# Joining two factors on VectorE, splitting with the bias, and moving the residual's scaling to GpSimd at one layer boundary

## The reference

```
# end of the first block, 512 tokens, 2048 channels
x = (ALPHA1*xl + g*out - mu) * rsqrt(var + eps) * ln_g + ln_b     # layer norm
# start of the second block
h    = x * (1 + scale) + shift
proj = h @ w_in_2            # q k v gate, glu_a glu_b g_conv
...
x = layer_norm(ALPHA*x + gate*y)                                  # x is needed again: the residual
```

## Time and profile before

| | |
|---|---|
| three runs | 3251.26, 3254.66, 3254.66 us, median 3254.66 |
| the profiled execution | 3252.81 us, its span 3251.2 us |
| mean granted TensorE clock | 0.994 |
| TensorE matmuls busy | 3180.1 us, 98% |
| VectorE busy | 2236.8 us, 69% |
| ScalarE busy | 1346.4 us, 41% |
| GpSimd busy | 294.1 us, 9% |
| moved | 556.41 MB, 171 GB/s |

### The profile page before, as it was taken

How to read it: one execution, slowest core, us unless ns; L and a number is a source line. 1 busy time by engine, 2 the same in 40 slices (tenths; PEclk the granted TensorE clock), 3 DMA queues, 4 the chain that set the end, 5 groups by cost and what they waited for, 6 DMA issues and landing times.

```text
span 3251.2 us, 47549 instructions
## 1 busy us (share of the span) xinstructions
PE 3180.1 (98%) x16736; PEld 2607.7 (80%) x16736; DVE 2236.8 (69%) x3562; ACT 1346.4 (41%) x2085; POOL 294.1 (9%) x521
## 2 busy tenths in 40 slices
PE   7999999999999999999999999999998999999997
PEld 4799999888777777889888777777786888788886
DVE  3488778766777776687556777774676999655446
ACT  2435564432444445246322444444326222454423
POOL 0000002011011101100101000000112000000002
PEclk9999999999999999999999999999999999999999
DMA  9765558556444444655755444432553322222333
GB/s 398 285 237 200 201 187 298 195 207 217 158 149 158 152 138 165 230 176 200 260 192 196 154 147 139 161 113 81 205 211 129 130 90 100 90 86 88 104 118 103
DMA packets 112092, 556.41 MB, mean 171 GB/s; under 512 B 17984, under 2 KB 22128, under 8 KB 69072
## 3 DMA queue, kind: packets, MB, share of 16 engines
q1 hardware_dynamic: 52000, 350.25, 30.2%
q0 software_dynamic: 59952, 204.29, 18.8%
HBM read 531.33 MB, written 23.09 MB: 171 GB/s over the span
## 4 chain that ended last, share of the span: by engine, by line
PE 80%; DVE 9%; DMA 4%; ACT 3%; issue 2%; DVEq 2%; ACTq 0%; POOLq 0%; POOL 0%; SPq 0%
PE acc L1453 23%; PE acc L1455 22%; PE acc L1454 22%; PE pv L1640 3%; DVE w_lo L2026 2%; PE S L1614 2%; DMA xy<-in_wm 2%; PE S L1629 1%; DMA gates<-in_wm 1%; DVE gates L2079 1%; DMA raw<-in_w 1%; PE misc L1543 1%; ACT w_hi L746 1%; ACT work L746 1%; DVE vtok L2079 1%
## 5 line engine op out<-in xcount | busy, mean ns | idle before, releaser
L1453 PE MATMUL acc<-h_hi,w_hi 128*128 128x512 f32 (+1 forms) x4448 | 1623.1, 365 | 12.9 <-DVE w_lo L2026 9.0
L1455 PE MATMUL acc<-h_hi,w_lo 128*128 128x512 f32 (+1 forms) x4448 | 1593.1, 358 | 0.0
L1454 PE MATMUL acc<-h_lo,w_hi 128*128 128x512 f32 (+1 forms) x4448 | 1591.4, 358 | 0.0
L1453 PEld LDWEIGHTS acc<-h_hi,w_hi 128*128 128x128 f32 x4448 | 841.3, 189 | 161.1 <-issue 34.1
L1454 PEld LDWEIGHTS acc<-h_lo,w_hi 128*128 128x128 f32 x4448 | 841.9, 189 | 124.7 <-issue 6.7
L1455 PEld LDWEIGHTS acc<-h_hi,w_lo 128*128 128x128 f32 x4448 | 841.0, 189 | 124.6
L2026 DVE TENSOR_TENSOR w_lo<-raw,w_hi 128x1024 fp32r<-128x1024 f32 x584 | 689.1, 1221 | 178.4 <-ACT w_hi L746 174.2
L746 ACT ACTIVATE w_hi<-raw 128x1024 fp32r<-128x1024 f32 x584 | 585.3, 1053 | 66.0 <-PE acc L1508 18.5
L746 ACT ACTIVATE ev<-acc 128x512 f32<-128x512 f32 (+1 forms) x202 | 106.9, 533 | 804.4 <-PE acc L1455 788.9
L541 POOL DMA_DIRECT2D gates<-in_wm x288 | 153.7, 534 | 1363.7 <-DVE gates L2079 1238.8
L746 ACT ACTIVATE work<-S,small 128x768 f32<-128x768 f32 (+1 forms) x160 | 129.1, 814 | 257.7 <-DVE small L2195 257.7
(11 more groups left out here) (308 smaller groups left out, 2673.1 us busy)
## 6 DMA issues: line engine op xcount, KB each, us to landing
raw<-in_w SPq DMA_DIRECT2D x288, 1024.0 KB, 5.0
gates<-in_wm POOLq DMA_DIRECT2D x288, 512.0 KB, 4.8
xy<-in_wm SPq DMA_DIRECT2D x32, 1024.0 KB, 11.2
raw<-in_wp SPq DMA_DIRECT2D x4, 1024.0 KB, 12.6
x_d<-xy POOLq DMA_DIRECT2D x1, 4096.0 KB, 15.3
qb<-x_d POOLq DMA_DIRECT2D x16, 256.0 KB, 4.1
kb<-x_d POOLq DMA_DIRECT2D x16, 256.0 KB, 4.7
bias_d<-kb POOLq DMA_DIRECT2D x8, 384.0 KB, 20.2
```

The lines of the kernel that those rows point to most:

```text
L1453: mm(o, w_hi[:, w], h_hi[:, x], start=n == 0, stop=False)
L1454: mm(o, w_hi[:, w], h_lo[:, x], start=False, stop=False)
L1455: last = mm(o, w_lo[:, w], h_hi[:, x], start=False, stop=n == len(ks) - 1)
```

## The change

For each of the 16 tiles at this boundary VectorE now multiplies by gain and inverse deviation in one instruction and writes the product to a bank of `S` (four buffers); ScalarE only adds the bias while rounding into `h_hi`; VectorE adds the bias again while subtracting `h_hi` for `h_lo`. The whole modulated tile is written nowhere. The x tiles stay unscaled, and GpSimd multiplies them by a copy of the inverse deviation in `qb` (it can't read PSUM), which ScalarE makes by a second Exp. GpSimd's subtraction of the mean starts at tile 2 instead of 4. The half weight split moves ahead of the statistics. The loops over pairs on VectorE and ScalarE become straight code.

```diff
-        whole_glu = (S[:, 2 * SEQ:3 * SEQ], S[:, 3 * SEQ:4 * SEQ])
+        scaled_glu = [S[:, SEQ * n:SEQ * (n + 1)] for n in (2, 3, 0, 1)]
@@ GpSimd
-            for k in range(4, KT):
+            for k in range(2, KT):
                 x = tile(xy, k, SEQ)
                 nc.gpsimd.tensor_tensor(x, x, t1[:], ALU.subtract).then_inc(rest_done, 1)
+            pool.wait_ge(b_dev_kept, shown(b_dev_kept, 1))
+            for k in (*range(8, KT), *range(8)):
+                x = tile(xy, k, SEQ)
+                pool.wait_ge(n_ready, shown(n_ready, LN_AT["b"] + k + 1))
+                nc.gpsimd.tensor_tensor(x, x, qb[:], ALU.mult).then_inc(b_normed, 1)
@@ ScalarE, norm_affine
-                    act.wait_ge(n_ready, shown(n_ready, At(LN_AT[c] + 1, 1, i)))
+                    if c == "b":
+                        act.wait_ge(b_normed, shown(b_normed, At(-7 if first >= 8 else 9, 1, i)))
+                    else:
+                        act.wait_ge(n_ready, shown(n_ready, At(LN_AT[c] + 1, 1, i)))
@@ ScalarE, boundary
                     inverse_deviation("b", pv)
+                    f(qb[:], t2[:], ACT.Exp, scale=-0.5).then_inc(b_dev_kept, 1)
-            modulate("g.h", lambda i: tile(xy, i, SEQ), SEQ, lambda k: vec("c0", k), lambda k: vec("c1", k),
-                     normed=LN_AT["b"], to=whole_glu)
+            for k in range(KT):
+                act.wait_ge(n_ready, shown(n_ready, LN_AT["b"] + k + 1))
+                f(inputs("g.h", h_hi, k), scaled_glu[k % 4], ACT.Identity, bias=vec("c1", k)).then_inc(hhi_done, 1)
@@ VectorE, end of project_out
                     dve.sem_inc(ssum_ready, 1)
+                    if c == "b":
+                        lo(At(TILE0["glu"] + 1), (1,))
@@ VectorE, boundary
-                    for k in range(4):
+                    for k in range(2):
                         x = tile(xy, k, SEQ)
                         stt(x, stats[0], -1.0 / D, x, ALU.mult, ALU.add)
             dve.wait_ge(ln_sd, shown(ln_sd, LN_NO["b"] + 1))
             dve.drain()
-            scaled(0, 2, pv)
-            def next_pair(i):
-                dve.wait_ge(rest_done, shown(rest_done, At(-2, 2, i)))
-                scaled(i * 2, 2, pv)
-                modulated("g.h", SEQ, i - 1, whole_glu)
-            loop(dve, 1, 4, next_pair)
-            lo(At(TILE0["glu"] + 1), (1,))
-            loop(dve, 4, KT // 2, next_pair)
-            modulated("g.h", SEQ, KT // 2 - 1, whole_glu)
+            def scaled_and_gained(k):
+                if k >= 2:
+                    dve.wait_ge(rest_done, shown(rest_done, k - 1))
+                stt(scaled_glu[k % 4], tile(xy, k, SEQ), vec("c0", k), pv[:, :], ALU.mult, ALU.mult).then_inc(n_ready, 1)
+            def shifted_low(k):
+                dve.wait_ge(hhi_done, shown(hhi_done, H_AT["g.h"] + k + 1))
+                stt(inputs("g.h", h_lo, k), scaled_glu[k % 4], vec("c1", k), inputs("g.h", h_hi, k).bitcast(F32),
+                    ALU.add, ALU.subtract).then_inc(hlo_done, 1)
+            scaled_and_gained(0)
+            scaled_and_gained(1)
+            for k in range(KT):
+                shifted_low(k)
+                if k + 2 < KT:
+                    scaled_and_gained(k + 2)
```

More of the change, by code:

```diff
@@ L297, in build @@
         n_ready = sem("n_ready")
+        b_dev_kept = sem("b_dev_kept")
+        b_normed = sem("b_normed")
         x_ready = sem("x_ready")
```

## The result

| | before | after |
|---|---|---|
| median | 3253.11 us (18 runs, 3249.54 to 3255.11) | 3260.26 us (18 runs, 3258.00 to 3262.57) |
| ratio | | 1.0022, 95% interval 1.0016 to 1.0028 |
| profiled execution, its span | 3252.81, 3251.2 us | 3258.00, 3256.4 us |

The change makes the kernel 7 us slower (5 to 9 by the interval). I had forecast 3249.0, in a range up to 3255.

What follows compares the result with a forecast made beforehand. TensorE bounds the kernel, its matmuls filling 98% of the span. The profiled 3252.81 less 4.8 plus 0.1 already in the dates gave 3248.0, the median of runs 3249.9; the middle, 3249.0, was taken, range 3245.5 to 3255.

Steps and rivals of the forecast that it cites:

- Start and pace: At the boundary: first factor product starts at 2471.05, 0.9 earlier; VectorE's new instructions follow at 0.67, 1.34 us per tile.
- The moved split: Half weight split ahead of VectorE's statistics: 0.14 late for the mean, counted as +0.1 us.
- The sign that I had named: Before the first product, TensorE's wait for `h_lo` would be 4.8 instead of 6.7 us if the forecast was right.
- First matmul with all inputs ready: TensorE's third weight tile would start at 2498.05 instead of 2502.83, a gain of 4.8 us.
- Low clock hidden at the start: TensorE's first blocks: two slow ones from 2473.54 end at 2476.7, the next two fit before k = 4.
- Splits of the third weight tile: On VectorE beside GpSimd's multiplications: up to 1.24 each, first half ready by 2496.4, needed by TensorE at 2498.05.
- Rival C: VectorE's new instructions wait for GpSimd's running one, 1.26 per spacing: 12.4 us slower, 3266; chance 0.05.
- The store and the first taps: GpSimd's first store goes at 2505.4 or so, lands in about 5 us, with 5 us of cover before ScalarE's taps.
- VectorE's free time: At the first taps, VectorE's tenth of free time would take in any shortfall of the store's cover; nothing counted.
- The timed size: Whole kernel: a gain of 4.8 us, time 3249.0, counted as within what a measurement can't tell from no change.

Runs made afterwards that it cites:

- two pauses: Changed kernel with GpSimd resting before tiles 14 and 4 until the third and fourth weight tiles are split, first store moved ahead of the second rest; 3249.49 against 3252.82 us.
- two drains: Changed kernel with a GpSimd drain before its multiplications of tile 14 and of tile 4; 3249.97 against 3254.55 us.
- the six changed versions: Changed kernel without GpSimd's multiplications, or with one pause, two pauses, a drain after each, one short rest or two drains; ratios to the kernel before 0.9987 to 0.9995.
- one version: Changed kernel with one GpSimd wait before its seventh multiplication (tile 14) until the third weight tile is split; ratio 0.9992 to the kernel before.
- the one without multiplications: Changed kernel with GpSimd's 16 multiplications left out, their semaphore still counted; 3248.99 us against 3253.97.
- small kernels: Separate kernels computing nothing of the reference: VectorE weight splits asked for during GpSimd bursts of 6, 24 or 30; plain bursts of 30 gave 2.27 or 19.35 us.
- eight more reads: Kernel before with eight more GpSimd subtractions (two SBUF inputs, results unused) behind its twelve; ratio 1.0023.
- a drain after each: Changed kernel with a GpSimd drain after each multiplication; ratio 0.9995 to the kernel before.

## Why the prediction was wrong

- **Start and pace: right.** First product 5.39 us after GpSimd's start (forecast 2473.54 - 2468.2 = 5.34), 0.66 per instruction (0.67). VectorE's write to PSUM costs nothing that shows, and reading from there neither. The moved split delayed the mean by 0.2 us as forecast (0.14, though the terms that I gave add up to 0.07), but only against an execution whose sums ran at the lower clock, as the one did that I read. Against sums at 1.00 it is 1.1 us. The sign that I had named, a wait of TensorE for `h_lo` of 4.8 us instead of 6.7, hangs on the same thing: 6.5 in the profile of the changed kernel, whose sums ran at 1.00, and 4.8 in the two versions whose sums ran slow (two pauses, two drains).
- **First matmul with all inputs ready: right but for the split.** Forecast 29.85 after GpSimd's start; 29.74 to 29.77 in the six changed versions in which the split isn't kept out.
- **Low clock hidden at the start: right.** By the same 29.75. The forecast did not have its return after the wait.
- **"Splits of the third weight tile (2494 to 2497) meet the multiplications, at up to 1.24 each ... ready by 2496.4": the step that failed.** I took one instruction of GpSimd's as the most that a VectorE instruction waits. It waited for ten. The two rows that I went by had the split asked for in the last instruction of its burst, where one instruction's wait is all that can be seen, or an addition inside a burst of five, which the later runs show to be too short. That the conflict exists I had; how long it lasts I had from nothing, and I gave it no bound from above. The rows for that bound were there: GpSimd's own end, 2505.4 in my dates, plus 1.22 = 2506.6 against a need of 2498.05, so 8.6 us of wait (measured 8.6), and 2.0 for the clock. GpSimd's row of the burst of five, in the kernel before:

```profile
3230.76 2.87 POOL L739 TENSOR_SCALAR xy<-xy,vecs 128x256 f32<-128x256 f32 x5 [2.95 <-DVE xy L2574]
```

- **Rival C: the right place, the wrong instruction.** I looked for the conflict in the new pair, whose one SBUF tensor plus per-channel operand doesn't conflict (0.66 beside a busy GpSimd), and not in the old split behind it, which had got a busy neighbour.
- **The store and the first taps:** the store went at 2504.5, near my 2505.4. Its cover is thin, though. Pausing GpSimd used it up, 4.1 us of wait in one version, and VectorE's free time didn't take that in as I had said: the version ends 2.7 us later than the one without multiplications.
- **The timed size.** -4.8 forecast; the profile has +5.9, being -5.0 + 8.8 (the third tile's delay, nearly all of it the wait) + 2.1 (clock and the like). The 18 timed runs have +7.2, which the interval (5 to 9) joins to it.

The Trainium skill ("SBUF — State Buffer", "Who interferes with whom") has the shared port held for a whole instruction by whoever comes first, the other blocking. The rows of the small kernels agree for up to 14 of GpSimd's instructions since a rest or drain (2.35 us at most, against 1.21 alone). From 15 on the next instruction too goes ahead of VectorE, to the end of the burst (28.5 us at most). The measurement decides.

## What to carry to other kernels

When work moves to an idle engine, look not only at whether that engine keeps up and at the instructions written for it, but at every instruction that shares a port with it and now runs at the same time; put the end of the whole burst, not one instruction, as the upper bound. A long GpSimd burst with SBUF reads wants a drain or a short rest every ten instructions or so, placed ahead of the moment at which VectorE has two-SBUF-input work that TensorE waits for. And a wait of TensorE costs more than itself: here 8.6 us brought 2 more at the lower clock.

## What the runs showed of the hardware

- A VectorE instruction with two SBUF inputs, asked for while GpSimd runs instructions with SBUF inputs back to back, gets in after the running one if that is at most the 15th since GpSimd's last rest or drain, and after the burst's end otherwise: 2.27 against 19.35 us for a 1.21 us instruction. That holds in all 206 trials of the four small kernels but for one detail: asked for 0.05 us before a hand-over, the split once let the next instruction pass too (2.35 us). Width, form, met waits and what VectorE did before don't move the border; the phase was tried in bursts of six and after 11, not at the border. Why it is so isn't shown. In the full kernel no run has a split asked for in the 13th to 20th instruction; up to the 10th they got in, in the 21st it was kept out, and one asked for in the 12th, with eight more reads behind it, was kept out too, against the rule.
- A drain behind a long row costs more than one behind a short row: 2.15 us of idle time after 20 instructions with the two drains and after 15 with a drain after each, 0.16 or 0.17 after one, six or seven.
- GpSimd memsets, and VectorE instructions with one tensor in SBUF and one in PSUM, with or without a per-channel operand, don't take part in the conflict: with memsets behind the last subtraction the split took 1.42 us where reads made it 9.37, and the new pair kept its spacing of 0.66 beside a GpSimd that is never idle.
